# Preparing both parts of the output weights in the projection stage, and ScalarE's output copies ahead of its DMA issues

## The chip, the cores and the metric

The kernel runs on one core of one Trainium2 chip. The metric is the device time of one execution in microseconds (us); lower is better. Five engines work side by side and meet only at semaphores: TensorE (PE, matrix products), VectorE (DVE), ScalarE (ACT), GpSimd (POOL) and SyncE (SP, which issues DMAs). ScalarE issues some DMAs too.

## The reference, cut to what matters

One layer of a hybrid decoder, for a prompt of 4096 tokens with 16 learned tokens ahead, and 8 samples of 8 tokens. One input projection feeds two branches: sliding-window attention, and a state-space branch of 32 channel groups (16 channels, 64 complex states each). Their outputs are joined by one output projection.

```python
z = rmsnorm(x, norm_w) @ w_in                   # q, k, v, gate, u, g_ssm
...
y = Re(C scan(B u)) + D u                       # state-space branch
g = gelu(y)
s = g * sigmoid(g @ w_glu + b_glu)
s = rmsnorm(s * silu(g_ssm), ssm_out_norm_w)
a = rmsnorm(attn_o * silu(g_attn), attn_out_norm_w)
return x + concatenate([a, s]) @ w_out
```

The matrices `w_glu` (512 x 512) and `w_out` (1024 x 1024) are the "output weights" of the title. The output norms' weights are folded into `w_out` as a factor for each row.

## The kernel before, in words

Every large product is made in three parts so that float32 accuracy is kept: a matrix W is split into a high part (W rounded to the type fp32r) and a low part (W minus the high part), the data likewise, and TensorE adds high x high, high x low and low x high.

Four stages follow one another:

1. Attention, with the first part of the input projection (to about 736 us).
2. `early_projections` (736 to 1117 us): u and the state-space gate, in ST = 9 turns `s` of SW = 464 columns, 8 blocks `m` of 24 matmuls a turn. PSUM holds 7 blocks, so a block waits until VectorE has emptied the one seven before it (`z_out`). For the turn after, SP loads x in four pieces into `XT`, ScalarE makes the high part (`high_x`, L694), VectorE the low part (`low_x`, L820). VectorE empties the blocks (`u_out`, `gate_in`), ScalarE does a tanh of each gate block, VectorE finishes it (`gate_out`) and SP stores it (`store_g`). Between, VectorE computes parameters (`discretize`, in turns 0 to 3). In turns 2, 5 and 8 SP stores u, 696 KB for each of 4 blocks (`store_u`). GpSimd makes 16 phasor tables of eight instructions in two buffers, SP stores them in turns 4 to 7.
3. `state_space` (1117 to 1292 us): HG = 16 pairs `p` of channel groups. TensorE goes `direct(p)`, `chunk_inputs(p + 2)`, `from_states(p)`, `matrices(p + 3)`. VectorE goes `turn_inputs`, `scan_inputs`, `scan`, `turn_back`, `states` for pair p + 2 and then `vectors(p + 4)`. ScalarE copies results out of PSUM and issues the loads of the Toeplitz matrices (`MALL`) and the stores of the kernels (`kp`). SP loads u, parameters and tables and stores y. The output weights are also made here: SP loads 20 pieces of 128 x 512 (256 KB, `load_weight`) into a ring of four, two in each of the iterations p = 2 to 11. ScalarE scales a piece and makes the high part (`high_weight`, L2002 and L2004), and GpSimd subtracts for the low part (`low_weight`, L1914).
4. `late_projections` (from 1292 us): the GLU product and the output projection with these weights.

All queues are written out by hand and each engine takes its instructions strictly in order: one that waits holds up all behind it on that engine. In ScalarE's loop the order is:

```python
sample_states(p + 1); sample_copies(p + 1)
load_toeplitz(act, p + 2)      # waits until the kernel p + 2 is stored
groups.sample_inputs(act, p + 3, USA)
groups.diagonals(act, p + 4)   # waits for the parameters of pair p + 4
final_states(p)
for n in weights_of(p): high_weight(n)
y_copies(p)                    # TensorE's direct(p + 1) waits for these
groups.kernel_copy(act, p + 3, ...); groups.store_kernel(...)
groups.input_copy(act, p + 3)
```

`chunk_inputs(p)` waits for `sample_copies(p - 1)` (`vs_out`) and `input_copy(p)` (`w_out`), `direct(p)` for the Toeplitz load of pair p and the copies of pair p - 1, `matrices(p)` for `vectors(p)`, and `turn_inputs(p)` for `chunk_inputs(p)`.

## Time and profile before

| | |
|---|---|
| median of 3 runs | 1764.29 us (1764.03 to 1764.9) |
| the profiled execution's own time | 1761.64 us |
| its span, first to last instruction | 1759.8 us |
| mean granted clock of TensorE | 0.982 |
| busy: PE, DVE, ACT, POOL | 95%, 67%, 35%, 20% |

The profiled execution is 1.84 us longer than its span and 2.65 us shorter than the median of the runs. Busy shares are means over four stages that differ; what bounds a stage has to be read in that stage.

### The profile page before, as it was taken

To read this page: it belongs to the slowest core of one execution; us is meant where nothing else is said; L and a number is where in the kernel's file an instruction comes from. 1 tells how busy PE (TensorE), PEld (TensorE's weight loads), DVE (VectorE), ACT (ScalarE), POOL (GpSimd) and SP (SyncE) were. 2 spreads that over 40 slices of the span, in tenths; PEclk is the share of its full clock that TensorE was granted. 3 is DMA by queue.
4 is the path that set the end of the run, shared out by engine and by line. 5 is a ranking of instruction groups with operands and counts; after the bars stand their busy time and mean duration, and the time that the engine had idled before them with its cause. 6 is when DMAs were issued, how large, how long until landed. Compare 5 with 4: busy or idle time off the path is not lost. (4 is left out here: it accounts for less than half of the span.)

```text
span 1759.8 us, 24710 instructions
## 1 busy us (share of the span) xinstructions
PE 1676.1 (95%) x8604; PEld 1348.9 (77%) x8604; DVE 1185.1 (67%) x2652; ACT 623.8 (35%) x1631; POOL 345.9 (20%) x425
## 2 busy tenths in 40 slices
PE   6899999999999999699999999888899999999999
PEld 5677777787777777488888888555577888888886
DVE  7787888767878788666644334799956655466532
ACT  5455454544454554422111110245442222122210
POOL 1122222212222222100014452022211111111110
PEclk9999999999999999899999999999999999999999
DMA  6311111113312210323743816666674456354331
GB/s 230 124 64 64 64 64 64 64 66 123 107 64 78 69 40 13 110 69 94 127 111 83 154 52 134 147 209 204 189 156 143 110 132 154 128 137 111 112 118 63
DMA packets 197420, 191.16 MB, mean 109 GB/s; under 512 B 118064, under 2 KB 153520, under 8 KB 197296
## 3 DMA queue, kind: packets, MB, share of 16 engines
q1 hardware_dynamic: 192448, 184.86, 37.9%
q10 hardware_dynamic: 4848, 4.72, 0.9%
q8 instruction: 69, 1.13, 0.3%
q14 instruction: 55, 0.45, 0.1%
HBM read 131.81 MB, written 57.73 MB: 108 GB/s over the span
## 5 line engine op out<-in xcount | busy, mean ns | idle before, releaser
L1165 PE MATMUL ps_b<-b_WH,b_XH 128*128 128x512 f32 (+1 forms) x776 | 286.9, 370 | 0.8 <-issue 0.4
L1167 PE MATMUL ps_b<-b_WH,b_XL 128*128 128x512 f32 (+1 forms) x776 | 277.4, 357 | 0.0
L1166 PE MATMUL ps_b<-b_WL,b_XH 128*128 128x512 f32 (+1 forms) x776 | 277.1, 357 | 0.0
L1165 PEld LDWEIGHTS ps_b<-b_WH,b_XH 128*128 128x128 f32 x776 | 148.7, 192 | 28.8 <-issue 9.3
L1167 PEld LDWEIGHTS ps_b<-b_WH,b_XL 128*128 128x128 f32 x776 | 148.5, 191 | 21.6
L1166 PEld LDWEIGHTS ps_b<-b_WL,b_XH 128*128 128x128 f32 x776 | 149.1, 192 | 18.7
L1120 POOL TENSOR_TENSOR b_XL<-b_XT,b_XH 128x1024 fp32r<-128x1024 f32 x33 | 80.2, 2430 | 379.3 <-ACT b_XH L1364 307.8
L1430 ACT ACTIVATE b_SM<-ps_b,b_small 128x128 f32<-128x128 f32 x256 | 113.9, 454 | 113.0 <-DVE b_small L1613 110.4
L795 PE MATMUL ps_g<-w_X0H,w_nextH 128*128 128x464 f32 x320 | 122.5, 383 | 2.6 <-DVEq L847 2.6
L797 PE MATMUL ps_g<-w_X0H,w_nextL 128*128 128x464 f32 x320 | 120.2, 376 | 0.0
L796 PE MATMUL ps_g<-w_X0L,w_nextH 128*128 128x464 f32 x320 | 119.9, 375 | 0.0
L2444 DVE SCALAR_TENSOR_TENSOR l_OUT<-ps_g,l_small,l_OUT 128x512 f32<-128x512 f32 (+1 forms) x66 | 48.9, 749 | 100.8 <-PE ps_g L2350 100.8
L1766 PE MATMUL ps_g<-W_OUTH,l_AH 128*128 128x512 f32 (+1 forms) x264 | 105.7, 400 | 3.8 <-POOL l_AL L1780 3.8
L1767 PE MATMUL ps_g<-W_OUTL,l_AH 128*128 128x512 f32 (+1 forms) x264 | 104.6, 396 | 0.0
L1768 PE MATMUL ps_g<-W_OUTH,l_AL 128*128 128x512 f32 (+1 forms) x264 | 104.3, 395 | 0.0
L2348 PE MATMUL ps_g<-W_OUTH,l_SH 128*128 128x512 f32 (+1 forms) x264 | 102.9, 390 | 0.0
L2350 PE MATMUL ps_g<-W_OUTH,l_SL 128*128 128x512 f32 (+1 forms) x264 | 102.7, 389 | 0.0
L2349 PE MATMUL ps_g<-W_OUTL,l_SH 128*128 128x512 f32 (+1 forms) x264 | 102.7, 389 | 0.0
L840 DVE TENSOR_TENSOR e_TG<-ps_g,e_RXB 128x464 f32<-128x464 f32 x36 | 22.9, 642 | 110.9 <-PE ps_g L797 91.8
L795 PE MATMUL ps_g<-e_XH,w_nextH 128*128 128x464 f32 x256 | 97.0, 379 | 0.0
L797 PE MATMUL ps_g<-e_XH,w_nextL 128*128 128x464 f32 x256 | 95.5, 373 | 0.0
L796 PE MATMUL ps_g<-e_XL,w_nextH 128*128 128x464 f32 x256 | 95.2, 372 | 0.0
(339 smaller groups left out, 3637.9 us busy)
## 6 DMA issues: line engine op xcount, KB each, us to landing
b_XT<-in_xb SPq DMA_DIRECT2D x33, 512.0 KB, 4.0
b_XR<-in_x SPq DMA_DIRECT2D x33, 512.0 KB, 4.7
w_XT<-in_xt SPq DMA_DIRECT2D x36, 464.0 KB, 5.0
l_X<-in_xr SPq DMA_DIRECT2D x32, 512.0 KB, 4.6
out_out<-l_OUT SPq DMA_DIRECT2D x32, 512.0 KB, 3.0
scr_gs<-e_TG SPq DMA_DIRECT2D x36, 232.0 KB, 2.1
scr_u<-w_ST SPq DMA_DIRECT2D x12, 696.0 KB, 12.9
g_U<-scr_u SPq DMA_DIRECT2D x64, 130.5 KB
```

The source lines that it names most:

```text
L795: pe.matmul(bank(s, m), high, XH[s % 2][:, k, :], start=(k == 0), stop=False)
L796: pe.matmul(bank(s, m), high, XL[s % 2][:, k, :], start=False, stop=False)
L797: mm = pe.matmul(bank(s, m), low, XH[s % 2][:, k, :], start=False, stop=(k == KD - 1))
L1165: pe.matmul(bank[:, 0:c1 - c0], XH[b][:, k, :], WH[:, k, c0:c1], start=(k == 0), stop=False)
L1166: pe.matmul(bank[:, 0:c1 - c0], XH[b][:, k, :], WL[:, k, c0:c1], start=False, stop=False)
L1167: mm = pe.matmul(bank[:, 0:c1 - c0], XL[b][:, k, :], WH[:, k, c0:c1], start=False, stop=(k == KD - 1))
L1430: exped.mark(act.activation(SM[:, h, :], scores_of(g)[:, j, t % 2, :], ACT.Exp, bias=NM[:, h:h + 1], scale=RQX[:, h:h + 1], accum_out=SUM[ ...
L1766: pe.matmul(o, a_hi, high[:, c, cols], start=(c == 0), stop=False)
L1767: pe.matmul(o, a_hi, low[:, c, cols], start=False, stop=False)
L1768: mm = pe.matmul(o, a_lo, high[:, c, cols], start=False, stop=(c == 3))
L2348: pe.matmul(bank, lh, w[0], start=first, stop=False)
L2349: pe.matmul(bank, lh, w[1], start=False, stop=False)
```

## The change

In the projection stage, the second half of `XT` no longer holds x: two x pieces take turns in the first half, and the second half holds one raw weight piece (`RAW`), its high part (`HI`) and its low part (`LOW`). In each of the turns 1 to 4, five pieces are loaded, scaled and rounded by ScalarE, subtracted by GpSimd, and both parts are stored to device memory (`scr["w"]`); each piece reuses the buffers of the one before. Since x has only two buffers, the last two of its four pieces are loaded within the turn, and VectorE makes their low parts after `u_out(s, 1)`. In the state-space stage, ScalarE's and GpSimd's work on weights is gone: SP loads the high parts where it loaded the raw pieces, and ScalarE issues loads of the low parts. ScalarE's final states, output copies, kernel copy and store and input copy stand ahead of its Toeplitz loads, sample inputs, diagonals and weight loads.

```diff
@@ early_projections @@
+        RAW, HI, LOW = (XT[:, 4:8, :].rearrange("p k q -> p (k q)")[:, 512 * i:512 * i + 512] for i in range(3))
+        def weight_at(s, place):
+            return 5 * (s - 1) + place if 1 <= s <= NW // 5 else None
+        def piece(p):
+            return pieces(XT, p % 2)
...
@@ SP
                 def load_x(s, p):
-                    sp.wait_ge(x_lo, NPC * (s - 1) + p + 1)
-                    sp.dma_start(pieces(XT, p), I["xt"][s, :, 2 * p:2 * p + 2, :]).then_inc(x_ld[p], 16)
+                    if s >= ST:
+                        return
+                    sp.wait_ge(x_lo, NPC * s + p - 1)
+                    sp.dma_start(piece(p), I["xt"][s, :, 2 * p:2 * p + 2, :]).then_inc(x_ld[p], 16)
...
+                def store_weight(n):
+                    sp.wait_ge(ow_hi, n + 1)
+                    sp.dma_start(scr["w"][0, n], HI).then_inc(ow_st, 16)
+                    sp.wait_ge(ow_lo, n + 1)
+                    sp.dma_start(scr["w"][1, n], LOW).then_inc(ow_st, 16)
+                def next_weight(n):
+                    if n is None:
+                        return
+                    if n:
+                        store_weight(n - 1)
+                    sp.dma_start(RAW, out_weight(I, FAC, n)[0]).then_inc(ow_ld, 16)
...
                     for m in range(4):
-                        if s + 2 < ST:
-                            load_x(s + 2, m)
+                        load_x(s + 1 if m < 2 else s + 2, (m + 2) % 4)
+                        if m != 2:
+                            next_weight(weight_at(s, min(m, 2)))
                         store_u(s, m)
...
                     for m in range(4):
+                        if m in (0, 2):
+                            next_weight(weight_at(s, 3 + m // 2))
                         store_g(s, m)
...
@@ ScalarE
+                def high_weight(n):
+                    if n is None:
+                        return
+                    factor = out_weight(I, FAC, n)[1]
+                    act.wait_ge(ow_ld, 16 * (n + 1))
+                    act.activation(RAW, RAW, ACT.Copy, scale=factor).then_inc(ow_sc, 1)
+                    act.wait_ge(ow_sc, n + 1)
+                    if n:
+                        act.wait_ge(ow_lo, n)
+                        act.wait_ge(ow_st, 32 * n - 16)
+                    act.activation(HI.bitcast(F32R), RAW, ACT.Copy).then_inc(ow_hi, 1)
...
                         diagonals(s + 1)
-                        for p in range(NPC):
+                        for p in range(2):
                             high_x(s + 1, p)
...
+                        high_weight(weight_at(s, 0))
+                        for p in range(2, NPC):
+                            high_x(s + 1, p)
+                        high_weight(weight_at(s, 1))
                         rows(s + 1)
+                        high_weight(weight_at(s, 2))
...
                         tanh(s, m)
+                        if m in (0, 2):
+                            high_weight(weight_at(s, 3 + m // 2))
...
@@ GpSimd
+                def low_weight(n):
+                    pool.wait_ge(ow_hi, n + 1)
+                    if n:
+                        pool.wait_ge(ow_st, 32 * n)
+                    pool.tensor_tensor(LOW.bitcast(F32R), RAW, HI, ALU.subtract).then_inc(ow_lo, 1)
+                for n in range(NW - 5):
+                    low_weight(n)
                 pool.wait_ge(par.done, 1)
...
                 for p in range(HG):
+                    if p < 5:
+                        low_weight(NW - 5 + p)
...
@@ VectorE
-                        for p in range(NPC):
+                        for p in range(2):
                             low_x(s + 1, p)
...
                     u_out(s, 1)
+                    if s + 1 < ST:
+                        for p in range(2, NPC):
+                            low_x(s + 1, p)
                     u_out(s, 2)
...
@@ state_space @@
+        def load_weight(e, n, part):
+            e.dma_start(weight(n, part), scr["w"][part, n]).then_inc(w_ld[part], 16)
...
                     for n in weights_of(p + 1):
                         if n >= 2:
-                            load_weight(n)
+                            load_weight(sp, n, 0)
...
@@ GpSimd
-                for p in range(HG):
-                    for n in weights_of(p):
-                        low_weight(n)
-                    if p == 14:
-                        for t in range(2):
-                            ahead.low(pool, t, P)
+                for t in range(2):
+                    ahead.low(pool, t, P)
...
@@ ScalarE
                         sample_copies(p + 1)
+                    final_states(p)
+                    y_copies(p)
+                    if p + 3 < HG:
+                        groups.kernel_copy(act, p + 3, KP[(p + 3) % 2])
+                        groups.store_kernel(act, p + 3, KP[(p + 3) % 2])
+                        groups.input_copy(act, p + 3)
                     if p + 2 < HG:
                         load_toeplitz(act, p + 2)
                     if p + 3 < HG:
                         groups.sample_inputs(act, p + 3, USA)
                     if p + 4 < HG:
                         groups.diagonals(act, p + 4)
-                    final_states(p)
-                    for n in weights_of(p):
-                        high_weight(n)
-                    y_copies(p)
-                    if p + 3 < HG:
-                        groups.kernel_copy(act, p + 3, KP[(p + 3) % 2])
-                        groups.store_kernel(act, p + 3, KP[(p + 3) % 2])
-                        groups.input_copy(act, p + 3)
+                    for n in weights_of(p + 1):
+                        load_weight(act, n, 1)
```

## Rows read from the trace of the kernel before

**Rows 1.** Windows: length, busy PE, PEld, DVE, ACT, POOL us; clock, DMA share, GB/s
```profile
750.00:800.00 50.00, 50.00 (x236) 43.94 (x235) 36.49 (x116) 12.79 (x23) 0.00 (x0) 1.00 0.32 78
1150.00:1200.00 50.00, 40.45 (x261) 25.83 (x261) 49.21 (x63) 26.42 (x91) 13.72 (x10) 1.00 0.68 220
```

**Rows 2.** The same, cut where VectorE starts a pair (L2048 on PSUM)
```profile
1143.84:1152.99 9.15, 9.15 (x64) 6.30 (x64) 8.98 (x15) 3.69 (x17) 0.00 (x0) 1.00 0.49 145
1152.99:1164.29 11.30, 9.60 (x64) 6.06 (x60) 11.13 (x15) 5.47 (x21) 2.84 (x2) 1.00 0.76 236
...
1250.72:1261.54 10.82, 8.66 (x54) 5.53 (x54) 10.65 (x14) 5.73 (x22) 2.68 (x2) 1.00 0.66 210
```

**Rows 3.** VectorE's groups in the pair without GpSimd work, 1143.8 to 1153
```profile
L2075 DVE TENSOR_TENSOR_SCAN g_ZS<-g_PAR,g_Z 128x257 f32<-128x257 f32 x2 | 1.3, 678 | 0.0
L2048 DVE TENSOR_TENSOR g_TI<-ps_g,g_CS_last 128x1028 f32<-128x1028 f32 x1 | 1.2, 1229 | 2.4 <-PE ps_g L518 2.4
...
L2057 DVE TENSOR_TENSOR g_Z<-g_TI 128x257 f32<-128x257 f32 x1 | 0.4, 428 | 0.0
...
L2058 DVE TENSOR_TENSOR g_Z<-g_TI 128x257 f32<-128x257 f32 x1 | 0.4, 420 | 0.0
```

**Rows 4.** The same groups over the ten pairs after it, 1152.9 to 1261.5
```profile
L2075 DVE TENSOR_TENSOR_SCAN g_ZS<-g_PAR,g_Z 128x257 f32<-128x257 f32 x20 | 16.9, 884 | 0.0
L2058 DVE TENSOR_TENSOR g_Z<-g_TI 128x257 f32<-128x257 f32 x10 | 11.7, 1169 | 0.0
...
L2057 DVE TENSOR_TENSOR g_Z<-g_TI 128x257 f32<-128x257 f32 x10 | 9.6, 960 | 0.3
```

**Rows 5.** Groups of the state-space stage, 1105 to 1325
```profile
L1914 POOL TENSOR_TENSOR W_OUTL<-l_Y,W_OUTH 128x512 fp32r<-128x512 f32 x16 | 21.6, 1352 | 64.1 <-ACT W_OUTH L2004 64.0
...
L2002 ACT ACTIVATE l_Y<-l_Y,g_NO 128x512 f32<-128x512 f32 x16 | 11.3, 706 | 0.0
...
L2004 ACT ACTIVATE W_OUTH<-l_Y 128x512 fp32r<-128x512 f32 x16 | 10.1, 630 | 0.5
```

**Rows 6.** ScalarE and its DMA issues in order of time (start us, us)
```profile
1136.00 0.48 ACT L487 ACTIVATE g_BD<-g_PAR 64x32 f32<-64x32 f32 x2 [6.43 <-DMA g_PAR<-in_ssm_d]
...
1179.97 0.31 ACTq L543 DMA_DIRECT2D scr_kp<-g_KP  x1
...
1184.32 1.21 ACTq L1848 DMA_DIRECT2D g_MALL<-scr_kp  x2
```

**Rows 7.** TensorE in order of time, near the start of the state-space stage
```profile
1137.19 0.93 PE L1935 MATMUL ps_g<-g_U,g_MALL 128*128 128x272 f32 x2 [2.38 <-ACT l_YSS L1990]
...
1143.63 2.05 PE L1949 MATMUL ps_g<-g_S,g_CP 64*128 64x272 f32 x16
```

**Rows 8.** DMA issues in the state-space stage: KB each, us to landing
```profile
l_Y<-in_w_out SPq DMA_DIRECT2D x16, 256.0 KB, 6.5
...
l_GS<-scr_gs SPq DMA_DIRECT2D x8, 256.0 KB, 3.6
```

**Rows 9.** DMA issues in turn 2 of the projections, 825 to 863
```profile
scr_u<-w_ST SPq DMA_DIRECT2D x4, 696.0 KB, 12.6
w_XT<-in_xt SPq DMA_DIRECT2D x4, 464.0 KB, 9.6
```

**Rows 10.** ScalarE in order of time, in turns 1 to 3 of the projections
```profile
822.82 0.59 ACT L714 ACTIVATE e_TH<-e_TG 128x464 f32<-128x464 f32 x1 [2.37 <-DVE e_TG L840]
...
824.45 3.57 ACT L694 ACTIVATE e_XH<-w_XT 128x928 fp32r<-128x928 f32 x4
843.13 0.56 ACT L707 ACTIVATE e_RXB<-ps_g 128x464 f32<-128x464 f32 x1 [15.11 <-PE ps_g L782]
...
884.33 0.56 ACT L707 ACTIVATE e_RXB<-ps_g 128x464 f32<-128x464 f32 x1 [14.93 <-PE ps_g L782]
```

**Rows 11.** GpSimd in order of time: the first instruction of two phasor tables
```profile
888.71 0.62 POOL L761 TENSOR_TENSOR w_ST<-phasors 128x256 f32<-128x256 f32 x1 [146.04 <-DVEq L326]
...
892.91 0.63 POOL L761 TENSOR_TENSOR w_ST<-phasors 128x256 f32<-128x256 f32 x1
```

More of the change, by code:

```diff
@@ L693, in high_x @@
                         act.wait_ge(z_full, NB * (s - 1))
-                    act.activation(pieces(XH[s % 2], p), pieces(XT, p), ACT.Copy).then_inc(x_hi, 1)
+                    act.activation(pieces(XH[s % 2], p), piece(p), ACT.Copy).then_inc(x_hi, 1)
                 def diagonals(s):
@@ L873, in _ @@
                     if s + 1 < ST:
-                        for p in range(NPC):
+                        for p in range(2):
                             low_x(s + 1, p)
@@ L1811, in state_space @@
         END = sb("END", [P, HG, 2, 8])
-        NO, WARM = sb("NO", [P, KD]), sb("WARM", [P, 1])
+        WARM = sb("WARM", [P, 1])
         (WUH, WUL), (WOH, WOL) = W3
-        STG = [ahead.Y0[:, i, :, :].rearrange("p t q -> p (t q)") for i in range(4)]
-        const_ld, halved, zeroed, warm = groups.const_ld, sem("norm_halved"), sem("pads_zeroed"), sem("gelu_ready")
+        zeroed, warm = sem("pads_zeroed"), sem("gelu_ready")
         p_ld, u_ld, cs_ld = groups.p_ld, groups.u_ld, groups.cs_ld
         m_ld, y_st = [sem(f"toeplitz_ld{i}") for i in range(RM)], ahead.y_st
-        w_ld, w_sc, w_hi, w_lo = [sem(f"w_ld{i}") for i in range(4)], sem("w_scaled"), sem("w_high"), sem("w_low")
+        w_ld = [sem("w_high_ld"), sem("w_low_ld")]
         mats = groups.mats
@@ L1826, in tile, with weight @@
             return Tile(None, p)
-        def weight(n):
+        def weight(n, part):
+            glu, out = (W3[0][part], W3[1][part])
             if n < 4:
-                return I["w_glu"][n * P:(n + 1) * P, :], 1.0, WUH[:, n, :], WUL[:, n, :]
+                return glu[:, n, :].bitcast(F32)
             k, h = (n - 4) // 2, (n - 4) % 2
-            c = slice(512 * h, 512 * h + 512)
-            return I["w_out"][k * P:(k + 1) * P, c], NO[:, k:k + 1], WOH[:, k, c], WOL[:, k, c]
-        NW, W_FROM = 20, 2
+            return out[:, k, 512 * h:512 * h + 512].bitcast(F32)
+        W_FROM = 2
         def weights_of(p):
@@ L1909, in _ @@
                     pool.memset(k[:, 0:P], 0.0).then_inc(zeroed, 1)
-                def low_weight(n):
-                    _, _, high, low = weight(n)
-                    pool.wait_ge(w_hi, n + 1)
-                    pool.tensor_tensor(low, STG[n % 4], high.bitcast(F32), ALU.subtract).then_inc(w_lo, 1)
-                for p in range(HG):
-                    for n in weights_of(p):
-                        low_weight(n)
-                    if p == 14:
-                        for t in range(2):
-                            ahead.low(pool, t, P)
+                for t in range(2):
+                    ahead.low(pool, t, P)
             @block.tensor
@@ L1962, in _ @@
                 pe.wait_ge(w_out, HG)
-                pe.wait_ge(w_lo, NW)
+                for ld in w_ld:
+                    pe.wait_ge(ld, 16 * NW)
                 pe.wait_ge(turned, HG)
@@ L1997, in final_states @@
                     act.activation(XS[:, p, :, 8:9], S[p % 2][:, :, NC:N], ACT.Copy).then_inc(f_out, 1)
-                def high_weight(n):
-                    _, factor, high, _ = weight(n)
-                    act.wait_ge(w_ld[n % 4], 16 * (n // 4 + 1))
-                    act.activation(STG[n % 4], STG[n % 4], ACT.Copy, scale=factor).then_inc(w_sc, 1)
-                    act.wait_ge(w_sc, n + 1)
-                    act.activation(high, STG[n % 4], ACT.Copy).then_inc(w_hi, 1)
                 sample_copies(0)
```

36 lines of the change are left out of this document (22 added, 14 removed).

## The prediction

> **What bounds the kernel now.** I read the page first: TensorE is busy for 95% of the span, but in the slices of the state-space stage it is at its lowest and VectorE at its fullest. The windows of a stage each make that plain: in the projections TensorE has no idle time (50.00 of 50 us) and VectorE has much; in the state-space stage VectorE is busy for 49.21 of 50 us and TensorE for 40.45 [rows 1]. So time is to be won in the state-space stage through VectorE, and the projection stage can only lose, if something keeps TensorE waiting.
>
> Next I cut the state-space stage where VectorE starts a pair. The pair from 1143.84 has no GpSimd work in it and takes 9.15 us. The next takes 11.30 with 2.84 us of GpSimd work, and the last of ten such pairs 10.82 [rows 2]. The ten run from 1152.99 to 1261.54, 108.55 us, 17.05 more than ten of 9.15. The groups say where it went. Alone, one half of the scan takes 678 ns, L2058 420 and L2057 428 [rows 3]; in the ten pairs 884, 1169 and 960 [rows 4]. That is 20 x 0.206 + 10 x 0.749 + 10 x 0.532 = 16.9 us, the whole excess. These are the instructions under which GpSimd's L1914 runs, 20 times, about 1352 ns each [rows 5]. VectorE is stretched by GpSimd; it does not wait for weights.
>
> **Part 1, weight work out of the state-space stage.** Removed: 20 GpSimd subtractions and 40 ScalarE activations (706 + 630 ns a piece [rows 5]). ScalarE's are worth nothing in themselves, since it is half idle there (5.47 of 11.30 us [rows 2]). The subtractions are worth up to 17.05 us, if nothing else needs more than 9.15 us for a pair. TensorE needs 8.66 busy of 10.82 at full clock [rows 2], so it fits. What stands against it are the next two parts.
>
> **Part 2, ScalarE's order.** At the start, ScalarE sits idle for 6.43 us behind the diagonals' parameters, and the output copies come after it; TensorE's direct(1) waits 2.38 us for these and VectorE then 2.4 us for chunk inputs [rows 6, 7, 3]. With the copies ahead, they follow from_states(0) at once: direct(1) can start at about 1134.9 and not 1137.19. Following chunk_inputs(3) through the new queue (kernel and input copies, two Toeplitz issues of 1.21 us together [rows 6], the diagonals when their parameters land at 1136.0, sample copies at about 1137.5) gives chunk inputs at 1139.5; VectorE, which no longer waits for final_states(0) behind the same parameters, finishes vectors(4) at about 1140.5 and starts the pair there instead of at 1143.84. Gain 3.3 us.
>
> In the steady state the order costs something. Let TensorE start matrices at M. About 1.25 us later ScalarE can copy the kernel. Then follow 0.8 us to the input copy (0.31 of it issue), 1.21 us of Toeplitz issue [rows 6], 0.7 for sample inputs and diagonals, and two weight issues of 0.45 each, which I put between the kernel store's 0.31 and a Toeplitz load's 0.6 [rows 6]. Sample states and copies end at about M + 5.1. TensorE's 8.66 us a pair [rows 2], less some 2 for from_states [rows 7] and 2 for chunk inputs, which are as many matmuls, bring it to chunk_inputs at M + 4.5, and it has to wait. With those 4 us behind it the loop closes at 9.1: just under VectorE's 9.15. No slack is left, so each tenth on ScalarE's queue counts. With 0.9 us for each of its four load issues it is 10.3. I take 9.45, the floor plus 0.3, as it is nearest to the issue times shown.
>
> **The transfers.** A pair moves 2.2 MB now; the low parts add 512 KB, about 2.75 MB in all. The DMA share is 0.66 to 0.76 of the longer pairs [rows 2], 7.1 to 8.6 us, and 512 KB at the rate that the first pair's row gives for a full share (145 / 0.49 = 296 GB/s [rows 2]) adds 1.8. That is 8.9 to 10.4 us for a pair: as much as VectorE needs or more. Bounds: hidden (9.15), or 2.75 MB at the 236 GB/s of the fastest row, 11.65. I take it as nearly hidden, since that row had a quarter of the engines' time left. A weight piece lands 6.5 us after its issue now [rows 8], and nothing waits for one until pair 16, so latency alone is free; only throughput and held-up issues count. The 0.3 above covers that.
>
> A rule that speaks against this part: the Trainium skill, DMA: Bandwidth & Descriptors, Issuing engines are not separate DMA queues, says that DMAs issued by different engines share the same 16 engines, so moving the low parts to ScalarE saves only issue time. By it, the added bytes come on top in full; by the share rows they still just fit. It is the second rival below.
>
> Sum for this stage: 3.3 + 108.55 - 10 x 9.45 = 17.3 us gained (20.3 at the floor, a loss of 4.7 at 11.65).
>
> **Part 3, what the projections take on.** Per weight: one load, two activations, one subtraction, two stores, in one ring position, so they form a chain: landing 3.6 us (a 256 KB load in a lighter stretch [rows 8]), ScalarE 1.4, GpSimd 1.4, SP's issue of the low store 0.45, and 0.1 for semaphores: 6.95 us. Five are 34.8 us. The turn adds about 3.3 us before the first load can be issued (SP's load stands behind an x load that waits for low_x, which follows the diagonals and a high part of 0.9 us [rows 10]) and about 2.3 us where the fourth and fifth wait for tanh, gate_out and gate stores: 40.4 us. A turn of TensorE is 41.2 us (843.13 to 884.33 [rows 10]). So ScalarE, SP and VectorE, which now have most of each turn free, become about as long as TensorE. Their lag behind the turn's start does not shrink any more.
>
> How much lag is allowed: VectorE must empty a block before TensorE comes to it seven blocks (36 us) later, and u_out(s, 0) now comes about 5.5 us after ScalarE's last tanh of the turn before. So the lag must stay under 30 us, and under about 25 in turn 3, where VectorE has 15 us of phasors in between. Before, the lag is about 1 us at turn 2 (last tanh at 822.82; the turn starts four blocks before 843.13, at about 822.3 [rows 10]). With the change I get 12 at turn 2, from the late start of the first weight behind SP's eight sample loads and the sines' table loads. Turn 2 stores u: x loads land after 9.6 us and u stores after 12.6 [rows 9] instead of 3.6 to 5, for two or three weights: +15, lag 27. Turn 3: about 25. Turn 4: the subtraction of weight 18 stands behind phasor table 2 (4.2 us [rows 11]), which waits for table 0's store, which SP issues behind weight 18's load: +3.6, lag 28. Then turn 5 stores u again and its last x piece lands late. TensorE would wait some 1.5 us in turn 3 and 1.5 near turn 5: I take 3 us. Bounds: 0, if a landing is 0.5 us shorter (2.5 us a turn); 20, if the stores of turn 2 double the landings of all five weights, since beyond the limit each us of lag is a us of time.
>
> GpSimd's 20 subtractions stretch VectorE here too, by about 0.85 us each as above, 4.3 us a turn; its idle time of 13 us in a 50 us window [rows 1] covers it. Without that cover it would be lag. The factor's load and two small activations cost nothing for the same reason.
>
> **Sum.** Profiled time 1761.64 - 17.3 + 3 = 1747.3 us. The profiled execution is 2.65 us under the median of the runs, so 1750.0.
>
> **Rivals.**
> - Likeliest, as summed: 1750, own range 1744 to 1757. Chance 0.55.
> - ScalarE's queue closes the state-space loop at 10.3 us. For it: the queues are fuller than in any row, and an issue behind a full queue holds ScalarE. Against: at a share of 0.67 two still take 1.21 [rows 6]. Gain 3.3 + 5.5 = 8.8, less 3: 1758.5. Chance 0.17.
> - The DMA engines bound the pair: at 10.6 us the gain is 3.3 + 2.55 - 3 and the time 1761.4, at 11.0 it is 1765.4. For it: no row above 236 GB/s [rows 2], 290 needed. Against: shares of at most 0.76. By the skill's rule above this is where it would go. Chance 0.13.
> - Slower: the weight chain in turns 2 to 5 holds SP and ScalarE so long that TensorE waits for `z_out` or x parts. It decides from 17.3 us of waits on, a lag of about 47 us; every weight of turns 2 to 4 landing after 5 to 6 us would do. Each restart may add some more: after 2.38 us idle, L1935's first two matmuls took 0.93 us [rows 7]. 25 us of waits give 1772. Against: loads are short outside turns 2 and 5. Chance 0.10.
> - The stretch moves elsewhere: VectorE stays at 10.85 a pair for another reason, and only 3.3 - 3 = 0.3 is left: 1764. Against: the 9.15 pair has none of it. Chance 0.05.
>
> **How the numbers follow.** About 0.2% (3.5 us) is what a measurement of this kernel can tell from no change. Faster than 1760.8: 0.55 + 0.17 + 0.05 of the third = 0.77. Same: 0.06 of the third and the fifth, 0.11. Slower: 0.02 + 0.10 = 0.12. The range from 1743 (floor, no waits, less a little for the clock) to 1763 leaves out most of the last three and little else.
>
> **What would show it.** Right: pairs of 9.2 to 9.7 us, scan halves at 678 and L2057 and L2058 near 430 throughout; the third pair starts some 3 us earlier after its stage's start; TensorE waits in `early_projections` sum to under 5 us. Wrong: chunk inputs waiting for L1981 by more than 1 us a pair (second case), direct waiting for MALL or U loads with DMA share near 1 (third), idle TensorE at L795 in turns 3 to 6 released by L832 or L820 (fourth).

## The result, and the profile after

The changed kernel takes 1777.79 us, the median of 5 runs (1771.86 to 1780.53), beside 1764.9 for the kernel before in the same session. The ratio is 1.0075, with a 95% interval of 1.0051 to 1.0098: slower by about 13 us, where 14 us faster was forecast. The profiled execution of after is the lowest of its five (1771.86 us, span 1770.0), so the traces differ by 10.2 us, and a usual run loses some 3 us more than what follows.

Cut at the same events, the two spans differ so. "Pair" is the stretch from one start of VectorE's product with the chunk inputs (L2048 before, L2106 after) to the next. The last row ends where VectorE first makes a low part for the gate.

| stretch | before, us | after, us | change |
|---|---|---|---|
| up to the first block of the projections | 736.2 | 734.9 | -1.4 |
| the nine turns of the projections | 377.0 | 388.8 | +11.9 |
| to the first pair, and pairs 0 to 2 | 30.6 | 26.7 | -3.9 |
| pairs 3 to 13 | 117.7 | 119.6 | +1.9 |
| pairs 14, 15 and the way to the gate | 31.8 | 34.0 | +2.2 |
| the last stage | 466.5 | 466.0 | -0.5 |

**The projections.** TensorE's waits over the whole stage have one line that the stage before does not have (both have one wait of 2.6 us besides):

```profile
PE ps_g L860 <- ACT e_DIAG L744: 8.1, 4, 6.9
```

It reads: TensorE, at the spread matmul of line 860, waited for ScalarE's diagonals of line 744, 8.1 us in four places, once 6.9. The long wait is TensorE's line below (start us, us, engine and line, then idle time and its releaser); after it stand, each in order of time, ScalarE, GpSimd and SyncE's DMA issues:

```profile
972.90 1.92 PE L860 MATMUL ps_g<-e_DIAG,e_ONES 128*128 128x464 f32 x2 [6.87 <-ACT e_DIAG L744]
```
```profile
958.33 0.72 ACT L765 ACTIVATE w_XT<-w_XT,e_FAC 128x512 f32<-128x512 f32 x1 [5.44 <-DMA w_XT<-in_w_out]
...
969.86 0.72 ACT L765 ACTIVATE w_XT<-w_XT,e_FAC 128x512 f32<-128x512 f32 x1 [7.81 <-DMA w_XT<-in_w_out]
970.61 0.63 ACT L770 ACTIVATE w_XT<-w_XT 128x512 fp32r<-128x512 f32 x1
971.15 0.57 ACT L758 ACTIVATE e_TH<-e_TG 128x464 f32<-128x464 f32 x1
971.63 1.22 ACT L744 ACTIVATE e_DIAG<-w_ID,w_RX 128x112 f32<-128x112 f32 x4
```
```profile
960.25 1.10 POOL L839 TENSOR_TENSOR w_ST<-phasors 128x256 f32<-128x256 f32 x1 [6.41 <-DMA scr_cs<-w_ST]
...
965.33 1.27 POOL L822 TENSOR_TENSOR w_XT<-w_XT 128x512 fp32r<-128x512 f32 x1
```
```profile
966.62 0.32 SPq L672 DMA_DIRECT2D scr_w<-w_XT  x1
966.98 0.43 SPq L679 DMA_DIRECT2D w_XT<-in_w_out  x1
```

The reader sees one ring position turned into a chain. The weight scaled at 958.33 has its high part by 959.7, but GpSimd's low part starts at 965.33, because a phasor table that had waited 6.41 us for a store stands ahead of it. SyncE stores that low part at 966.62 and only then loads the next weight. It lands at 969.86, ScalarE has waited 7.81 us for it, and tanh and the next diagonals stand behind it on ScalarE. The waits are 8.1 of the 11.9 us. Most of the rest is a slower clock behind them: 0.87 of full speed was granted in the window of the long wait, and its 143 recorded products took 33.13 us, where at the pace of the second window below they would take 30.2 (an estimate). In the seven other windows of a turn each, of which one stands here, it was 1.00 (columns as in [rows 1]):

```profile
940.00:980.00 40.00, 33.13 (x143) 28.38 (x142) 17.68 (x25) 11.30 (x20) 31.20 (x50) 0.87 0.48 163
...
1022.00:1063.00 41.00, 41.00 (x194) 36.25 (x194) 19.70 (x21) 10.00 (x16) 32.90 (x53) 1.00 0.44 138
```

**The state-space stage.** The windows of the two stages that [rows 1] shows, then the whole stretch of pairs 3 to 13 and five of its pairs (columns as there):

```profile
750.00:800.00 50.00, 50.00 (x236) 43.80 (x234) 33.39 (x113) 11.65 (x24) 0.00 (x0) 1.00 0.35 87
1150.00:1200.00 50.00, 42.84 (x254) 28.86 (x252) 44.30 (x70) 17.32 (x75) 0.00 (x0) 0.93 0.76 239
```
```profile
1150.42:1270.02 119.60, 99.25 (x602) 66.91 (x600) 99.47 (x155) 38.74 (x165) 0.00 (x0) 0.94 0.77 239
1150.42:1159.57 9.15, 8.37 (x58) 5.81 (x56) 8.98 (x15) 3.48 (x15) 0.00 (x0) 1.00 0.73 214
1159.57:1168.71 9.14, 8.85 (x60) 6.01 (x58) 8.97 (x14) 3.48 (x15) 0.00 (x0) 1.00 0.87 257
1168.71:1178.78 10.07, 8.29 (x56) 5.65 (x54) 9.06 (x14) 3.58 (x15) 0.00 (x0) 1.00 0.75 236
1178.78:1191.99 13.21, 9.63 (x53) 5.98 (x52) 9.07 (x14) 3.31 (x15) 0.00 (x0) 0.82 0.73 245
1191.99:1202.17 10.18, 9.41 (x56) 6.53 (x58) 9.07 (x14) 3.48 (x15) 0.00 (x0) 0.90 0.82 249
```

VectorE now has its 9.0 us of work in every pair, long or short, where a pair of [rows 2] had 11.13 and 10.65. So the stretch by GpSimd is gone, and VectorE's groups over the eleven pairs say it again, beside the 884, 1169 and 960 ns of [rows 4]:

```profile
L2133 DVE TENSOR_TENSOR_SCAN g_ZS<-g_PAR,g_Z 128x257 f32<-128x257 f32 x22 | 14.0, 678 | 0.0
...
L2106 DVE TENSOR_TENSOR g_TI<-ps_g,g_CS 128x1028 f32<-128x1028 f32 x8 | 9.8, 1229 | 3.7 <-PE ps_g L518 3.5
...
L552 DVE TENSOR_TENSOR g_WB<-g_PAR 128x512 f32<-128x512 f32 x11 | 7.6, 690 | 13.6 <-DMA g_PAR<-in_ssm_d 13.5
...
L2115 DVE TENSOR_TENSOR g_Z<-g_TI 128x257 f32<-128x257 f32 x11 | 4.7, 429 | 0.4
```

What VectorE saved it now waits: 13.5 us for parameters that have not landed, 8.8 for chunk inputs in the whole stage. The waits from the first pair to 1290 (us in all, times, longest), the costliest behind the buffers:

```profile
PE ps_g L518 <- ACT l_XS L2050: 23.3, 13, 4.6
DVE g_WB L552 <- DMA g_PAR<-in_ssm_d: 13.5, 7, 3.5
ACT g_BD L487 <- DMA g_PAR<-in_ssm_d: 13.1, 7, 3.7
ACT g_YS L2058 <- DMA scr_y<-g_YS: 11.6, 3, 4.2
DVE g_TI L2106 <- PE ps_g L518: 8.8, 7, 2.1
```

These chains end at transfers: parameters hold ScalarE's diagonals, the sample copies stand behind them, and TensorE's chunk inputs wait for those. The SyncE queue in order of time shows why parameters are late: its issues, 0.43 us each when nothing is in the way, take up to 2.88 (a single load of 65 KB).

```profile
1166.00 5.07 SPq L1942 DMA_DIRECT2D scr_y<-g_YS  x4
1171.11 1.67 SPq L1931 DMA_DIRECT2D W_OUTH<-scr_w  x2
1172.82 3.01 SPq L472 DMA_DIRECT2D g_U<-scr_u  x4
1175.94 2.88 SPq L454 DMA_DIRECT2D g_PAR<-scr_par  x1
1178.87 0.44 SPq L455 DMA_DIRECT2D g_PAR<-in_ssm_d  x1
...
1189.03 0.40 SPq L454 DMA_DIRECT2D g_PAR<-scr_par  x1
```

It is SyncE's queue that is held. Over pairs 3 to 13 the rows of its issues add up to 117.6 of 119.6 us, and to 90.7 of 117.7 in before, with nearly the same list of transfers (rows are merged, so what SyncE waits inside a group of four counts too). ScalarE's issues of the low parts keep the price that the prediction gave them, 0.44 us on average and 0.75 at most.

From the first pair to the gate, the DMA engines move 37.86 MB at a mean of 216 GB/s in after, and 32.61 MB at 187 in before.

### The profile page after: what moved, and what is told of

Its sections match the earlier page's. It is cut to its first block and busy times, and to the rows that moved or that the text cites. A ratio compares the mean times of both kernels' runs of the same rounds, so it can differ in the third digit from the quotient of the medians.

```text
span 1770.0 us, 24827 instructions
## 1 busy us (share of the span) xinstructions
PE 1682.2 (95%) x8604; PEld 1353.3 (76%) x8604; DVE 1178.6 (67%) x2652; ACT 628.9 (36%) x1631; POOL 344.0 (19%) x425
## 5 line engine op out<-in xcount | busy, mean ns | idle before, releaser
L1861 POOL TENSOR_TENSOR l_AL<-l_A,l_AH 128x512 fp32r<-128x512 f32 (+1 forms) x33 | 42.6, 1291 | 369.3 <-ACT l_AH L1857 369.3
L1847 PE MATMUL ps_g<-W_OUTH,l_AH 128*128 128x512 f32 (+1 forms) x264 | 105.3, 399 | 4.9 <-POOL l_AL L1861 4.9
```

The source lines that it names most:

```text
L1847: pe.matmul(o, a_hi, high[:, c, cols], start=(c == 0), stop=False)
```

## The experiments

Times are medians; a ratio is to the runs of the kernel before in the same session, with its 95% interval. Stretches come from one profiled execution of each. All start from the changed kernel unless said otherwise, and stretches are those of the table. The diffs are cut to their main lines; `...` marks what is left out.

**1. Low parts not loaded.** ScalarE's loads of the low parts are left out; GpSimd clears their tiles at the start of the stage, so the products with low parts of the output weights are zero.

```diff
+                for w in (WUL, WOL):
+                    pool.memset(w[:].bitcast(F32), 0.0).then_inc(cleared_low, 1)
...
-                    for n in weights_of(p + 1):
-                        load_weight(act, n, 1)
```

> The changed kernel without the 20 loads of low parts by ScalarE in the state-space stage (GpSimd clears the low parts once at the stage's start instead, so the low parts' share of the products is left out). The bytes of a pair fall back to those of before, 2.2 MB. Transfer theory (SP and the DMA engines can't move 2.75 MB in 9.15 us, so SP's issues are held up, parameters and stores land late, and all else waits for these): the pairs fall from 10.87 us on average to 9.15 to 9.4, the stage shortens by 16 to 18 us, the time from about 1777 to about 1760. Order theory (ScalarE's sample copies stand behind diagonals and load issues, transfers would have fitted): ScalarE's two weight issues go (0.9 us), but the rest of its queue stays; pairs of about 10, the time falls by some 9 us. Both leave the projection stage as it is (394 us from its first matmul to the first pair).

1763.34 us, 0.9999 (0.9977 to 1.0021). Pairs 3 to 13 took 107.11 us, 12.5 less than in after: eight of the pairs are 9.14 or 9.15, two 9.5 and 9.6, one 14.8. Projections 388.6 as in after. So the low loads (20, 5.2 MB) carry the loss of this stage, and without them most pairs are as forecast. The stage shortens by less than the 16 to 18 us of the transfer theory. SyncE's issues add up to 105.3 of the 107.11 us here too, so a busy queue alone is not the loss. Whether it lies in the bytes, the number of loads or the issuing engine is told apart in 10 and 13.

```profile
1153.00:1260.11 107.11, 95.06 (x602) 64.29 (x600) 99.01 (x154) 38.46 (x165) 0.00 (x0) 0.97 0.69 218
```

**2. Sample copies first.** The next pair's sample states and copies ahead of ScalarE's DMA issues, since TensorE waited for them.

```diff
+                sample_states(1)
+                sample_copies(1)
                 for p in range(HG):
-                    if p + 1 < HG:
-                        sample_states(p + 1)
-                        sample_copies(p + 1)
...
                     if p + 2 < HG:
+                        sample_states(p + 2)
+                        sample_copies(p + 2)
                         load_toeplitz(act, p + 2)
```

> The changed kernel with ScalarE's sample states and sample copies of pair p + 2 directly behind the input copy of pair p + 3, ahead of the Toeplitz loads, sample inputs, diagonals and weight loads: chunk_inputs no longer waits for a queue that waits for parameters. Order theory: the 23.3 us in which TensorE waits for L2050 vanish, VectorE's waits for chunk inputs (8.8 us) with them, pairs of 9.15 to 9.6, the time falls by 12 to 16 us. Transfer theory: TensorE's wait moves to other instructions (y copies, parameters, Toeplitz loads), pairs stay above 10.3, the time falls by under 5 us.

1774.63 us, 1.0067 (1.0038 to 1.0095); pairs 3 to 13 119.0. TensorE's wait for the copies is gone, and ScalarE waits 33.5 us for the stores of y in its place. The wait moved and the stage didn't shorten, as the transfer theory had it.

**3. Diagonals early.** In the projections, a turn's diagonals stand behind `rows` of the turn before, not behind its weights and tanh.

```diff
-                        diagonals(s + 1)
...
                         rows(s + 1)
+                        if s + 2 < ST:
+                            diagonals(s + 2)
                         high_weight(weight_at(s, 2))
```

> The changed kernel with ScalarE's diagonals for the row broadcast of turn s + 2 made in turn s behind rows(s + 1), so that TensorE's spread does not stand behind ScalarE's lag; all else as it is. If the lost 11 us of the projection stage are this wait and the slow matmuls after it, the stage falls from 394 us to 383 to 385 and the time by 8 to 11 us. If the lag then meets the next limit (z_out of u_out, seven blocks ahead, or the x parts), waits of TensorE for VectorE's L910 or L898 come up in turns 3 to 6 and the stage stays above 389.

1770.44 us, 1.0042 (1.0023 to 1.0062); projections 381.7, so 7.1 of the 11.9 us came back: between the two theories. What was left in the stage:

```profile
PE ps_g L875 <- DVE w_X0L L900: 2.2, 1, 2.2
PE ps_g L875 <- DVE w_ST L912: 1.7, 1, 1.7
```

The first is the low part of an x piece, the second a block that VectorE emptied late, since a late x piece stood ahead of it. Both fall where ScalarE waits for x pieces behind the stores of u of turn 5:

```profile
986.07 0.98 ACT L738 ACTIVATE w_X0H<-w_XT 128x928 fp32r<-128x928 f32 x1 [10.98 <-DMA w_XT<-in_xt]
994.36 0.98 ACT L738 ACTIVATE w_X0H<-w_XT 128x928 fp32r<-128x928 f32 x1 [7.31 <-DMA w_XT<-in_xt]
```

**4. Parameters first.** SyncE issues the parameters ahead of the loads of u.

```diff
-                    if p + 3 < HG:
-                        groups.load_u(sp, p + 3)
                     if p + 4 < HG:
                         groups.load_params(sp, p + 4)
                     if p + 3 < HG:
+                        groups.load_u(sp, p + 3)
                         groups.load_tables(sp, p + 3)
```

> The changed kernel with SP's loads of the parameters of pair p + 4 ahead of the loads of u of pair p + 3, which wait for y_full(p - 1). If late parameters are what the pairs suffer from (ScalarE waits 19.8 us for them at the diagonals, VectorE 13.5 at vectors), both waits vanish and the pairs fall to 9.5 to 10, the time by 9 to 14 us. If the transfers as a whole are the bound, the wait moves to u, y stores or Toeplitz loads, and the pairs stay above 10.3.

1778.25 us, 1.0084 (1.0056 to 1.0112); pairs 3 to 13 118.0. The pairs stay above 10.3 us, its second case; the waits changed places, to 38.4 us of ScalarE behind the stores of y.

**5. The order alone, on the kernel before.** ScalarE's new order with the old way of making the weights.

```diff
+                    final_states(p)
+                    y_copies(p)
...
                     load_toeplitz(act, p + 2)
...
-                    final_states(p)
                     for n in weights_of(p):
                         high_weight(n)
-                    y_copies(p)
...
```

> The kernel before with only the new order of ScalarE's work in the state-space loop (output copies ahead of its DMA issues, the high parts of the weights last). Theory one (the pairs of the kernel before are bound by the stretched GpSimd subtractions and by transfers, not by ScalarE's order): the order alone moves the time by under 2 us, 1762 to 1766 beside 1764; the ten slow pairs keep some 11 us. Rival A (the order is worth the 3 to 4 us that the prediction gave it): 1760. Rival B (the order is a part of the loss, because toeplitz loads and sample inputs are issued later): 1767 or more.

1773.77 us, 1.0072 (1.0044 to 1.0100): rival B. Pairs 3 to 13 took 130.16 us. Two things moved, as waits from the first pair to 1284 and VectorE's groups from 1162 to 1270 show:

```profile
PE ps_g L518 <- ACT l_XS L1981: 32.6, 13, 3.6
```
```profile
L562 DVE TENSOR_TENSOR g_CP<-g_Q 128x544 f32<-128x544 f32 x9 | 14.2, 1573 | 0.3
L558 DVE TENSOR_TENSOR g_Q<-g_PAR 128x544 f32<-128x544 f32 x9 | 11.8, 1314 | 0.0
...
L2057 DVE TENSOR_TENSOR g_Z<-g_TI 128x257 f32<-128x257 f32 x9 | 3.9, 429 | 0.3
```

The sample copies stand behind four activations of weights, 2.7 us, and TensorE waits for them 13 times. And GpSimd's subtractions fall on other instructions of VectorE: L2057 is at 429 ns again, while L558 takes 1314 and L562 1573 ns, where after has 718 and 725. So the stretch goes with the time of GpSimd's work and not with one instruction. Pairs 0 to 2, though, took 21.80 us and not 24.85, nearly the gain that the prediction gave the order.

**6. Other turns.** Experiment 3, and the weights made in turns 1, 3, 4 and 6 in place of 1 to 4, out of the turns that store u. GpSimd's subtractions 10 to 19 stand between other phasor tables for it.

```diff
+        TURNS = [1, 3, 4, 6]
-            return 5 * (s - 1) + place if 1 <= s <= NW // 5 else None
+            return 5 * TURNS.index(s) + place if s in TURNS else None
...
-                for n in range(NW - 5):
+                for n in range(NW - 10):
                     low_weight(n)
+                ahead_of = {0: [10], 1: [11], 2: [12, 13], 3: [14], 10: [15, 16, 17, 18], 11: [19]}
```

> The changed kernel with the diagonals of the next turn but one early (as in the third run) and the twenty weights made in turns 1, 3, 4 and 6 in place of 1 to 4, so that turns 2 and 5, which store u, have none. Theory one (after the diagonals, the late x loads behind the stores of u in turn 5 are the projections' next limit, 1.7 and 2.2 us of waits and a lower clock behind them): the projections come from 381 to about 377 us and the run to 1766. Rival (the traffic of the weights costs the same in any turn): 381 again, 1770.

1767.37 us, 1.0036 (1.0019 to 1.0052); projections 376.7, as in before (377.0), with no wait of TensorE in the stage. All of that stage's loss is gone. How much of the last 5.1 us is due to the turns and how much to the places of the subtractions, the run does not tell apart.

**7. Loads spread over the pairs.** One weight in most pairs in place of two in ten.

```diff
+        COUNTS = [2, 2, 1, 1, 1, 1, 1, 1, 0, 1, 1, 2, 2, 2, 2, 0]
```

> The changed kernel with the twenty loads of each part spread over the pairs: two weights in pairs 0 and 1, one in each of pairs 2 to 7, none in pair 8 (which stores the samples), one in 9 and 10, two in 11 to 14. Theory one (the pairs are bound by what the DMA engines move, 250 GB/s, and a pair with one weight carries 0.5 MB less, about 2.2 MB or 9 us): pairs 2 to 10 return to about 9.2 to 9.5 us, the last ones stay near 10 to 11; the stretch from pair 3 to 14 falls from 119.6 to about 110, the run to 1769. Rival A (bytes cost 4 us per MB wherever they stand): the stretch stays near 119, 1777. Rival B (the last pairs with two weights run late and delay the gate's operands): 1775 or more with a longer tail behind pair 14.

1776.98 us, 1.0085 (1.0054 to 1.0116). Pairs 3 to 13 took 109.1 us, 10.5 less, as theory one said, but pairs 14, 15 and the way to the gate took 42.7 and not 34.0: rival B took the gain back.

**8. Experiments 6 and 7 together**, with the edits of both.

> The three mendings together: diagonals early, weights in turns 1, 3, 4 and 6, loads spread over the pairs. Theory one (the two losses are separate, one in each stage, and add up): 1777 less 11 in the projections and less 9 in the state-space stage, 1757 to 1760, below the kernel before by 0.2 to 0.4%. Rival (the losses of the two stages are of one cause, the total traffic, and only move): 1768 or more.

1768.32 us, 1.0038 (1.0016 to 1.0059). Projections 376.8, pairs 3 to 13 108.4, the way to the gate 46.0: the rival. With 1767.37 in 6, spreading is worth nothing. Behind pair 14 ScalarE waits 17.7 us for the stores of y, where it waits 3.4 in 6.

**9. The old order, on the changed kernel.** With experiment 5 it closes a square.

```diff
+                    load_toeplitz(act, p + 2)
...
                     final_states(p)
+                    for n in weights_of(p + 1):
+                        load_weight(act, n, 1)
                     y_copies(p)
...
-                    load_toeplitz(act, p + 2)
```

> The changed kernel with ScalarE's old order in the state-space loop: its DMA issues ahead of the output copies, the loads of the low parts where the high parts of the weights were made. With the fifth run it makes a square of old and new order by old and new weights. Theory one (in the changed kernel the pairs are bound by transfers, whatever the order): pair 3 to 14 stays at 118 to 120 us, the run at 1776 to 1778. Rival (the new order costs some 10 us with either way of making the weights, as it did alone: TensorE's chunk inputs wait for the sample copies, which now stand behind the diagonals' wait for the parameters): the stretch falls to about 110, the run to 1768. Third possibility: the new order helps where no weights are made, and the old one costs 3 us or more: 1781.

1776.62 us, 1.0091 (1.0061 to 1.0122), pairs 3 to 13 121.1. The rival falls: the order costs only where weights are still made in the stage (5), and with them gone neither order is better. TensorE's 23.3 us behind the sample copies became 22.0 behind the output copies (L2003 <- L2059, 9 times).

**10. Low parts issued by SyncE**, the same bytes.

```diff
                         if n >= 2:
                             load_weight(sp, n, 0)
+                        load_weight(sp, n, 1)
...
-                    for n in weights_of(p + 1):
-                        load_weight(act, n, 1)
```

> The changed kernel with both parts of each weight loaded by SyncE, so that ScalarE issues none of them; the same bytes. Theory one (the bytes bind, not the engine that issues): 1775 to 1780, pair 3 to 14 at 118 to 121 us. Rival A (the issues hold ScalarE up, and that is what delays the sample copies): the stretch falls to 112, 1770. Rival B (SyncE's issues are the queue that is full; four weight loads a pair there delay the stores of y and the parameters more): 125 us, 1783.

1777.52 us, 1.0095 (1.0063 to 1.0127), pairs 3 to 13 118.5: theory one. The issuing engine doesn't matter here, and since SyncE makes 20 more issues in no more time, the price of an issue isn't what binds.

**11 and 12. Loads as early as possible** on experiment 8 (4, 3 and 2 weights in pairs 0 to 2, then one), with the new and with the old order.

```diff
+        COUNTS = [4, 3, 2, 1, 1, 1, 1, 1, 0, 1, 1, 1, 1, 1, 1, 0]
```

> As the eighth run (diagonals early, turns 1, 3, 4 and 6), but the loads lie as far ahead as possible: 4, 3 and 2 weights in pairs 0 to 2, where the DMA engines move 60 to 100 GB/s, one in each of the others, none in pairs 8 and 15. Theory one (bytes over 250 GB/s bind: the eighth run's 10 us gained in the pairs were lost again behind pair 14, because its late weights met the loads for the gate): the tail behind pair 14 comes back from 46 to about 35 us, pair 3 to 14 stays at 109, the run to 1757 to 1760. Rival (what is not loaded late is paid early: pairs 0 to 3 get longer by as much): 1768.

> The run before with ScalarE's old order. If the order costs by itself (the rival of the ninth run): 5 to 10 us less than the run before, 1750 to 1755. If transfers bind: the same as the run before within 2 us.

1765.85 us, 1.0032 (1.0012 to 1.0053), and 1765.02, 1.0021 (1.0003 to 1.0038). In 11, pairs 3 to 13 took 113.8 us and not 109, and the way to the gate 40.5 and not 35: nearer the rival. The early loads go out only from 1129 on, and the pair there moves 234 GB/s in 8 already, not 60 to 100. The old order of 12 gains 0.8 us, so the new one does not cost by itself: transfers bind. The stage from the first pair to the gate took 176.5 and 173.2 us, beside 175.1 in after and 174.3 in before. Wherever the low loads lie in the stage, it takes 173 to 178 us; without them (1) it took 162.6.

**13. The same number of low loads, an eighth of the bytes.** Each moves 64 of 512 columns, and the other columns of the low parts are zero.

```diff
+            if part:
+                e.wait_ge(cleared_low, 2)
+                e.dma_start(weight(n, part)[:, 0:64], scr["w"][part, n][:, 0:64]).then_inc(w_ld[part], 16)
+                return
```

> The changed kernel with each load of a low part cut to 64 of its 512 columns (GpSimd clears the rest at the start of the stage): the same number of loads and of descriptors, an eighth of the bytes, so the rest of the low products is zero. If bytes bind: as the first run, pair 3 to 14 at 107 to 110 us, the run at 1764 to 1767. If the number of loads or of descriptors binds: 118 to 120, the run at 1776 to 1778. Between: both have a share.

1765.23 us, 1.0023 (1.0003 to 1.0043), pairs 3 to 13 110.27. Of the 12.5 us of experiment 1, 9.3 come back with the bytes and 3.2 stay. The eighth that is still loaded, 0.66 MB, would be 1.6 us of these at 12.5 us for 5.24 MB (an estimate); the rest may be the number of loads. Bytes have most of it.

**14 and 15. Weights loaded behind the pairs.** Experiment 6, with eight (or four) of the weights that meet the state-space part of the output loaded in the last stage, where TensorE bounds; the pairs carry one weight in most.

```diff
                 load_y(1)
                 load_gs(1)
+                for n in LATE_W:
+                    k, h = (n - 4) // 2, (n - 4) % 2
+                    for part in range(2):
+                        sp.dma_start(W3[1][part][:, k, 512 * h:512 * h + 512].bitcast(F32), scr["w"][part, n]).then_inc(ahead.w_late[h], 16)
                 load_x(2)
```

> The eighth run's projections, and in the state-space stage only twelve weights, two in pairs 0 and 1, one in 2 to 7, 9 and 10; the eight that meet the state-space part of the output are loaded behind the first tiles' inputs of the last stage, where TensorE needs them 32 us later. Theory one (bytes bind the pairs and nothing else): pairs at 9.15 to 9.3 but for the one behind the samples' stores, 21.5 + 105 + 34 us where the changed kernel has 175.1, so the run at about 1752, faster than the kernel before by 0.5%. Rival (the bytes cost the same there, as late tiles wait for loads that stand behind these): 1763 to 1768.

> As the run before, but with four weights late and sixteen in the pairs (one each in 11 to 14 as well). Theory one: the last pairs and the way to the gate take some 5 us more than in the run before, 1756 to 1758. If late loads are what costs: faster than the run before, 1750 to 1753.

1763.54 us, 1.0019 (1.0008 to 1.0031), the rival of 14, and 1763.48, 1.0022 (1.0006 to 1.0037), which neither theory of 15 had. With eight late, the stage from the first pair to the gate took 165.2 us, 9 less than before, but the last stage took 474.7 and not 466.5. It lost them in one place (TensorE's waits, 1295 to 1420, of the run with eight):

```profile
PE ps_g L1854 <- POOL l_AL L1868: 11.9, 1, 11.9
```

It is the fourth tile's attention output, whose load stands on SyncE behind the sixteen weight loads; in before this wait is 3.8 us, with four late 7.1.

**16 and 17. That tile's load first.**

```diff
                 load_gs(1)
+                load_a(3)
+                load_x(2)
                 for n in LATE_W:
...
-                load_x(2)
...
-                        if t + 3 < NT:
+                        if 0 < t < NT - 3:
                             load_a(t + 3)
```

> The fourteenth run with the fourth tile's attention load and the third tile's x load ahead of the sixteen late weight loads. If the 11.9 us of TensorE's wait were the place in the queue: 1751 to 1755, faster than the kernel before by 0.3 to 0.6%. If the bytes cost the same wherever they go: the wait comes back at the next tile or at the state-space part of the first tile, 1761 to 1764.

> The fifteenth run with the same two loads ahead of the eight late weight loads. Place in the queue: 7 us less than 1763.5, 1756. Bytes: 1761 to 1764.

With eight late 1756.08 us, 0.9977 (0.9957 to 0.9997); with four 1760.94, 0.9999 (0.9978 to 1.0019). With eight late the wait is back to 2.9 us and the last stage to 466.7: it was the place in the queue. This is the one version here that beats the kernel before, by 4 us, with an interval that ends just below 1; its projections take 376.6 us, its way from the first pair to the gate 163.9. With four late the wait falls too, from 7.1 to 2.8 us, but the last stage takes 467.7 where it took 467.9, and the time is nearer the figure of "bytes"; why is open.

```profile
PE ps_g L2402 <- DVE l_GL L2461: 3.4, 1, 3.4
PE ps_g L1854 <- POOL l_AL L1868: 2.9, 1, 2.9
PE ps_g L2417 <- DVE l_SL L2479: 1.7, 1, 1.7
```

## Why the prediction was wrong

**Two terms failed, one in each stage.** The sum was 17.3 us gained less 3 lost; the traces have 3.9 gained up to pair 3, 1.9 and 2.2 lost behind it, and 11.9 lost in the projections.

- *The state-space stage, "I take 9.45, the floor plus 0.3".* This is the larger error: 17.3 us gained were forecast for the stage, 0.2 were lost. The step behind it read the DMA share: a row at 0.76 "had a quarter of the engines' time left", so 512 KB more would nearly fit. Pairs 3 to 13 took 10.87 us on average (119.6 / 11). Their mean rate, 239 GB/s, is that of the fastest pair of before (236), and the five pairs shown have 214 to 257 where 290 were needed. The bound from above in the prediction, 2.75 MB at 236 GB/s, was the right kind of reckoning, a little high in size: 119.6 us at 239 GB/s are 28.6 MB, 2.6 a pair. The rival of the DMA engines (chance 0.13) is what happened in this stage: experiment 1 shows it by leaving the loads out (12.5 us), 13 by their bytes (9.3), and 2, 4, 9 and 10 show that orders and issuers only move the wait. The queue that was held is SyncE's, for which the sum had no term; the text priced ScalarE's, whose issues cost what it said. By the Trainium skill, DMA: Bandwidth & Descriptors, Issuing engines are not separate DMA queues, DMAs started by different engines run on the same 16 DMA engines and interleave; the tenth run agrees, 118.5 us against 119.6.
- *The projections, "the lag must stay under 30 us".* 3 us were put down here, 11.9 were lost. The chain was priced well: the text named the subtraction behind a phasor table, and here it starts 5.6 us after its high part is done, where 3.6 was added, and ScalarE begins turn 5 at 971.63, 26 us behind TensorE's 945.7, where the text had 28. But the limit was taken from `z_out` and the x parts alone. ScalarE makes the diagonals of the next turn at the head of its own turn, and TensorE wants them for the spread some four blocks in, about 20 us by the 36 us for seven, not 25 to 30. The limit stood in [rows 10]: the copy at 843.13 waits for the spread, and the text itself puts the turn's start four blocks before it. So waits of 0.4 and 0.6 us come already before the long one. Experiment 3 moved the diagonals and gained 7.1 us; experiment 6 gained 5.1 more with the weights out of the turns that store u. The waits left by experiment 3 were for an x piece behind those stores and for a block that VectorE emptied behind one, the two limits that the text had, with 1.5 us near turn 5.

**What held.** GpSimd's stretch is as described: over all pairs L2115 and L2116 are at some 429 and 420 ns, and where the loads are away, pairs are at the 9.15 us of the free pair. The Trainium skill, SBUF — State Buffer, Who interferes with whom, has a VectorE instruction with two inputs in SBUF contend with a GpSimd one that reads SBUF; the trace agrees, and experiment 5 adds that the stretch follows GpSimd in time, to 1573 ns on L562. It was worth less than the 17.05 us of the text, though: without low loads, and so without either, pairs 3 to 13 take 107.1 us against 117.7 before, 10.6 less. One pair there takes 14.8 us (TensorE waits 5.8 of them; the parameters stand on SyncE behind the eight stores of the samples, 7.06 us of issue), and two take 9.5 and 9.6; the sum counted ten pairs as if each could be 9.15. In before, the pair with these stores takes 10.9 us like its neighbours, as SyncE has time to spare in pairs of 11 us. The 5.2 MB cost 12.5 us, a little more than the stretch was worth.

**The start** gained 3.3 us in pairs 0 to 2, as summed, but for less clear a reason: the order alone gave 3.05 (21.80 us, experiment 5), the weights alone 2.55 (22.30, experiment 9). Each does most of it, and only one of the two is needed.

**The order in the steady state** was rightly put at no slack. It didn't decide: what TensorE waited for behind it was late parameters, and with the old order it waited as long for output copies.

**The signs.** Of those for "wrong", the second case's came true, chunk inputs waiting for the sample copies (L2050 here, L1981 before) by 1.8 us a time, and pointed at ScalarE's queue. Experiments 2 and 10 show that it was not the cause. The third case, which happened, had as its sign waits for `MALL` and a share near 1; the trace has 1.9 us of such waits in pairs 3 to 13 and a share of 0.77. The fourth named other lines than the spread's.

**The rivals.** "Slower" was given to one mechanism, a weight chain with 17.3 us of waits or more (0.10). In fact it was the DMA rival of the state-space stage and a chain of half that size together. They were priced as if exclusive; the traces' other terms with the one alone give 1.7 us less than before, and the forecast gain with the other alone 5.4 less. The joint case had no chance of its own.

**What stays open.** Why spread or early loads lengthen the way to the gate by as much as they shorten the pairs (7, 8, 11) is seen as a sum; in 8 it goes with longer waits for the stores of y, but is not traced to one transfer. Half of the last 3.2 us of experiment 13 may be the number of loads. It is more than the stretch varies between executions: pairs 3 to 13 took 119.6, 119.5 and 120.1 us in after, 3 and 6, which have the same state-space stage.

## What to carry to other kernels

A share of DMA time below one is not room. Price added traffic by bytes over the highest rate that a stretch with the same mix of transfers has shown, and where that comes out at the length of the loop or above, count the bytes in full; then put them in a stage where TensorE bounds, behind the loads that the next tiles need. When an engine's queue gets a long chain, its allowed lag is the smallest over all that it makes for others: list each product and its consumer before a limit is named. And two rivals in two stages add up; give the case of both a chance.

## What the runs showed of the hardware

- The rate at a given share depends on what is moved. A pair of after has 257 GB/s at a share of 0.87, while 980 to 1022 of its projections, with the stores of u, has 144 at 0.87. No pair of after went past 258 GB/s; a stretch with weight and tile loads in the last stage of experiment 14 reached 299 at 0.93:

```profile
1300.00:1320.00 20.00, 19.04 (x87) 15.35 (x86) 12.76 (x12) 8.51 (x11) 4.38 (x3) 1.00 0.93 299
```

- Idle time costs TensorE twice. In the pair with 13.21 us the granted clock was 0.82 of full speed, behind a wait of 3.6 us; over pairs 3 to 13 it was 0.94 against 1.00 before, and the same matmuls took 99.25 us busy against 95.06 at 0.97 in experiment 1.
- A DMA issue is no fixed price: the same parameter load kept SyncE for 2.88 us at 1175.94 and 0.40 at 1189.03, while ScalarE's loads of 256 KB in the same pairs took 0.32 and 0.44.
